# A two-model transformer stack on one core: part of its transposes done by VectorE's 32x32 transposes and DMA copies instead of by TensorE

## The reference, cut to what matters

```python
# first model, one layer
h = h + rmsnorm(mixed attention, convolution and pooling @ w_out)
m = rmsnorm(h, norm_mlp_pre[i])
m = jnp.square(jax.nn.relu(jnp.einsum('bsd,df->bsf', m, w_up[i])))     # 4096 wide
m = jnp.einsum('bsf,fd->bsd', m, w_down[i])
h = h + rmsnorm(m, norm_mlp_post[i])
h = h + sigmoid(h @ ple_gate[i]) * (p[i] @ ple_proj[i])

# second model, one layer
x = x + 0.5 * rmsnorm_2(swiglu(rmsnorm_2(x), ffn1_w_in, ffn1_w_out))   # 2816 wide
proj = u @ w_in                        # xa, ya, q, k, v, g, sb, sc, sh, gates
oa = (ha * jax.nn.gelu(ya)) @ w_lru_out
ret = retention(q, k, v, positions)    # 4 heads of 512 values, each normalised
ob = (jax.nn.silu(g) * ret) @ w_ret_out
oc = (sb * causal_depthwise_conv(sc * sh, sc_conv_w)) @ w_sc_out
mixture = (ga * oa + gb * ob + gc * oc) @ w_out
x = x + rmsnorm_2(mixture)
x = x + 0.5 * rmsnorm_2(swiglu(rmsnorm_2(x), ffn2_w_in, ffn2_w_out))
```

## Time and profile before

| | before |
|---|---|
| device time, median of 3 runs | 2320.12 us (2319.9 to 2321.6) |
| span of the profiled execution, first to last instruction | 2318.0 us |
| PE busy | 2296.8 us, 99% |
| weight loads (PEld) | 1959.9 us, 85% |
| VectorE busy | 1540.9 us, 66% |
| ScalarE busy | 1221.5 us, 53% |
| GpSimd busy | 79.1 us, 3% |
| DMA, share of 16 engines | 56.4% for the queue of SP's DMAs |
| mean granted TensorE clock | 0.999 |

### The profile page before, as it was taken

The page is one execution under the profiler, slowest core; times in us unless marked ns, Lnnn a source line. Parts: engine busy times, 40 slices in busy tenths (PEclk is TensorE's granted clock), DMA queues, the critical chain, the costliest instruction groups (busy, mean ns, idle before and its releaser), DMA issues.

```text
span 2318.0 us, 30390 instructions
## 1 busy us (share of the span) xinstructions
PE 2296.8 (99%) x12124; PEld 1959.9 (85%) x12124; DVE 1540.9 (66%) x2019; ACT 1221.5 (53%) x1788; POOL 79.1 (3%) x134
## 2 busy tenths in 40 slices
PE   8999999999999999999999999999999999999998
PEld 6888888888888888988888888888889888888887
DVE  6867657776566667876575665665678765756664
ACT  6645446464455556755444554554567553445553
POOL 0110000100000000000000000000000000000000
PEclk9999999999999999999999999999999999999999
DMA  8437655456656555645665465565556456554652
GB/s 334 146 119 238 198 171 209 146 170 203 211 163 217 189 172 163 206 162 183 218 199 191 157 217 192 179 221 190 173 164 214 153 183 221 195 193 164 199 193 89
DMA packets 119805, 434.91 MB, mean 188 GB/s; under 512 B 13553, under 2 KB 13809, under 8 KB 119665
## 3 DMA queue, kind: packets, MB, share of 16 engines
q1 hardware_dynamic: 119664, 432.96, 56.4%
HBM read 431.86 MB, written 1.05 MB: 187 GB/s over the span
## 4 chain that ended last, share of the span: by engine, by line
PE 95%; DVE 4%; ACT 1%; issue 0%; POOL 0%; DMA 0%; DVEq 0%; POOLq 0%; ACTq 0%
PE ub L1716 21%; PE ub L1713 11%; PE ub L1684 9%; PE ub L1686 9%; PE ub L1685 9%; PE acc L1684 8%; PE acc L1685 8%; PE acc L1686 8%; PE ub L1691 1%; PE ub L1692 1%; PE ub L1693 1%; PE acc L1747 1%; DVE wlo L1020 1%; DVE work L1208 1%; PE acc L2162 0%; DVE best L1205 0%
## 5 line engine op out<-in xcount | busy, mean ns | idle before, releaser
L1020 DVE TENSOR_TENSOR wlo<-raw,whi 128x1024 fp32r<-128x1024 f32 x776 | 913.1, 1220 | 215.2 <-ACT whi L534 213.4
L534 ACT ACTIVATE whi<-raw 128x1024 fp32r<-128x1024 f32 x776 | 777.3, 1052 | 200.9 <-PE ub L1686 140.5
L1716 PE MATMUL ub<-xhl,whi 128*128 128x512 f32 x2176 | 514.6, 390 | 0.0
L1716 PEld LDWEIGHTS ub<-xhl,whi 128*128 128x128 f32 x2176 | 404.2, 188 | 82.7 <-issue 1.3
L1684 PE MATMUL acc<-whi,bhl 128*128 128x512 f32 x736 | 288.2, 392 | 0.0
L1685 PE MATMUL acc<-wlo,bhl 128*128 128x512 f32 x736 | 286.6, 389 | 0.0
L1686 PE MATMUL acc<-whi,bhl 128*128 128x512 f32 x736 | 286.5, 389 | 0.0
L1684 PE MATMUL ub<-whi,xhl 128*128 128x512 f32 (+1 forms) x704 | 275.3, 391 | 3.0 <-DVE wlo L1020 1.5
L1713 PEld LDWEIGHTS ub<-xhl,wlo 128*128 128x128 f32 x2176 | 272.0, 191 | 6.2
L1713 PE MATMUL ub<-xhl,wlo 128*128 128x256 f32 x2176 | 275.4, 283 | 0.0
L1686 PE MATMUL ub<-whi,xhl 128*128 128x512 f32 (+1 forms) x704 | 272.5, 387 | 0.0
(11 more groups left out here) (305 smaller groups left out, 2471.7 us busy)
## 6 DMA issues: line engine op xcount, KB each, us to landing
raw<-in_w SPq DMA_DIRECT2D x776, 512.0 KB, 5.0
gain<-in_gains SPq DMA_DIRECT2D x20, 512.0 KB, 7.8
tapw<-in_taps SPq DMA_DIRECT2D x16, 512.0 KB, 4.3
DEC<-in_decay SPq DMA_DIRECT2D x2, 768.0 KB, 8.1
par<-in_par SPq DMA_DIRECT2D x2, 647.0 KB, 9.4
par<-in_par SPq DMA_DIRECT2D x2, 556.0 KB, 7.2
H<-in_x SPq DMA_DIRECT2D x2, 512.0 KB, 4.5
out_h<-H SPq DMA_DIRECT2D x4, 256.0 KB, 2.6
```

What stands on the lines that cost most here:

```text
L534: do(act.activation(whi[:, s % RING, c], raw[:, slot, c], ACT.Copy), counts["w_hi"])
L1020: do(dve.tensor_tensor(wlo[:, s % RING, c], raw[:, PLACES[s][0], c], whi[:, s % RING, c].bitcast(f32), ALU.subtract), counts["w_lo"])
L1716: last = pe.matmul(bank, whi[:, s % RING, n:n + P], xhl[:, kt, :, :].rearrange("p a n -> p (a n)"), start=first, stop=stop, skip_group_che ...
```

## The change

The three functions that had PE transpose a tile (`turn_first`, `turn_p`, and the call of `turn_m(0)`) are removed from PE's list. In their place:

- VectorE transposes the 32x32 blocks of each 128x512 tile (`to_blocks`), one instruction for a tile, from `FH` to `FB`, from `tX` to `PB`, or from `MIX` to `MB`, and counts a semaphore (`blocked` or `pb`).
- SP waits for that semaphore between two weight loads and issues 16 DMAs (`move`), one for each pair of 32-partition groups. Each moves 32 partitions by 128 columns (of one or of two tiles) from one partition group to another, so that the sixteen blocks of a 128x128 tile stand where a full transpose has them. They land in `FH`, `PD` or `MD`, and count 256 on `moved0` or `moved1`.
- ACT and VectorE split the result as before, but read it in SBUF, with the blocks in another order (`moved_blocks`, `by_blocks`).

The moves are: two in each of the six feed-forwards (t=0, t=1), four in each layer's retention, and one in each layer's mixture: 22 moves, 352 DMAs. VectorE has 36 new transposes. On ACT, `turned_p(hd)` stands one chunk later than before, behind the squares of the next head. `turn_m(1)` stays on PE. The diff, cut (the wait indices of the other calls and the same edits for the second feed-forwards are left out):

```diff
@@ -176,6 +176,7 @@
+        FB = sb("FB", 0, at=unit(56), shape=[P, 4, 512])
@@ -259,6 +260,10 @@
+        PB = sb("PB", 0, at=unit(48), shape=[P, 2, 2048])
+        PD = sb("PD", 0, at=unit(16), shape=[P, 2, 2048])
+        MB = sb("MB", 0, at=unit(56), shape=[P, 2, 512])
+        MD = sb("MD", 0, at=unit(60), shape=[P, 2, 512])
@@ -294,6 +299,17 @@
+        def in_blocks(t):
+            return t.rearrange("p (c q i) -> p q c i", c=4, i=32)
+        def moved_blocks(t):
+            return t.rearrange("p (a q i) -> p q a i", a=4, i=32)
+        def by_blocks(t):
+            return t.rearrange("p q (a i) -> p q a i", i=32)
@@ -332,6 +350,15 @@
+                def move(event, dst, src, landed):
+                    done[event] += 1
+                    sp.wait_ge(sem[event], done[event])
+                    for a_ in range(4):
+                        for c in range(4):
+                            sp.dma_start(dst[32 * c:32 * c + 32, :, cols(a_)],
+                                         src[32 * a_:32 * a_ + 32, :, cols(c)]).then_inc(sem[landed], 16)
@@ -386,6 +413,10 @@
                             load_taps(L, 2, PIECES)
+                        if s == s1(L, "ffn", 7):
+                            move("blocked", FH[:, 0:4:2, :], FB[:, 0:4:2, :], "moved0")
+                        if s == s1(L, "ffn", 9):
+                            move("blocked", FH[:, 1:4:2, :], FB[:, 1:4:2, :], "moved1")
                         if s == s1(L, "ffn", 10):
@@ -400,6 +431,17 @@
+                        for name in ("f1", "f2"):
+                            if s == s2(L, name + "first", 7):
+                                move("blocked", FH[:, 0:1, :], FB[:, 0:1, :], "moved0")
+                            if s == s2(L, name + "first", 9):
+                                move("blocked", FH[:, 1:2, :], FB[:, 1:2, :], "moved1")
+                        for hd in range(RET_HEADS):
+                            if s == s2(L, "g", 0) + 2 * hd + 6:
+                                vs = slice(hd * 512, (hd + 1) * 512)
+                                move("pb", PD[:, :, vs], PB[:, :, vs], "moved0")
+                        if s == s2(L, "sco", 1) + 7:
+                            move("blocked", MD[:, :, :], MB[:, :, :], "moved0")
@@ -575,12 +617,12 @@
-                def first_hi(pieces):
-                    for b, t in pieces:
-                        nxt("tr_done")
-                        do(act.activation(bhi[:, 4 * b:4 * b + 4, cols(t)], quad(acc[:, 2 * b + t, :]), ACT.Copy),
-                           counts["hh"])
+                def first_hi(t, blocks_):
+                    nxt(f"moved{t}", 256)
+                    for b in range(blocks_):
+                        do(act.activation(by_blocks(bhi[:, 4 * b:4 * b + 4, cols(t)]), moved_blocks(FH[:, 2 * b + t, :]),
+                                          ACT.Copy), counts["hh"])
@@ -896,12 +938,18 @@
+                        nxt("moved0", 256)
...
-                            nxt("tr_done")
-                            do(act.activation(bhi[:, 4 * hd:4 * hd + 4, cols(t)], quad(acc[:, 3 - t, :]), ACT.Copy),
-                               counts["rph"])
+                            do(act.activation(by_blocks(bhi[:, 4 * hd:4 * hd + 4, cols(t)]),
+                                              moved_blocks(PD[:, t, hd * 512:(hd + 1) * 512]), ACT.Copy), counts["rph"])
...
+                        if fb == 0:
+                            nxt("moved0", 256)
+                            for t in range(2):
+                                do(act.activation(by_blocks(bhi[:, 8:12, cols(t)]), moved_blocks(MD[:, t, :]), ACT.Copy),
+                                   counts["mh"])
+                            return
@@ -956,23 +1004,25 @@
                             hd = j // 2
-                            if j % 2 == 0:
-                                if hd:
-                                    turned_p(hd - 1)
-                            else:
+                            if j % 2:
                                 used(s)
+                                act.wait_ge(sem["pb"], RET_HEADS * L + hd)
                                 for t in range(2):
...
                                 squares_o(hd)
+                                if hd:
+                                    turned_p(hd - 1)
                         elif kind == "ya":
                             if j == 0:
-                                turned_p(RET_HEADS - 1)
+                                act.wait_ge(sem["pb"], RET_HEADS * (L + 1))
                             sums_out(j, s, j % 2)
...
                             do(act.activation(two(bhi, 16 + 2 * j), tX[:, j % 2, :], ACT.Copy), counts["hh"])
+                            if j == 1:
+                                turned_p(RET_HEADS - 1)
                         elif kind in ("gb", "ga", "gc") and j % 2:
@@ -1028,13 +1078,26 @@
-                def first_lo(pieces):
-                    for b, t in pieces:
+                def rest_of(t, u, source):
+                    return dve.tensor_tensor(by_blocks(blo[:, u:u + 4, cols(t)]), moved_blocks(source),
+                                             by_blocks(bhi[:, u:u + 4, cols(t)].bitcast(f32)), ALU.subtract)
+                def first_lo(t, blocks_):
+                    for b in range(blocks_):
...
-                        do(dve.tensor_tensor(blo[:, 4 * b:4 * b + 4, cols(t)], quad(acc[:, 2 * b + t, :]),
-                                             bhi[:, 4 * b:4 * b + 4, cols(t)].bitcast(f32), ALU.subtract),
-                           counts["hid"])
+                        do(rest_of(t, 4 * b, FH[:, 2 * b + t, :]), counts["hid"])
+                def to_blocks(dst, source, count=None):
+                    return do(dve.transpose(in_blocks(dst), source.rearrange("p (q c i) -> p q c i", c=4, i=32)), count)
+                def first_blocks(t, blocks_):
+                    settle()
+                    for b in range(blocks_):
+                        to_blocks(FB[:, 2 * b + t, :], FH[:, 2 * b + t, :], counts["blocked"] if b == blocks_ - 1 else None)
@@ -1311,13 +1374,15 @@
                                 first(1, 0)
+                                first_blocks(0, 2)
                                 lo(sf + 4)
...
                                 first(1, 1)
-                                first_lo(((0, 0), (1, 0)))
+                                first_blocks(1, 2)
+                                first_lo(0, 2)
                         elif kind == "up":
@@ -1492,17 +1559,21 @@
+                        settle()
+                        for t in range(2):
+                            to_blocks(PB[:, t, hd * 512:(hd + 1) * 512], tX[:, t, :], counts["pb"] if t else None)
...
-                            do(dve.tensor_tensor(blo[:, 4 * hd:4 * hd + 4, cols(t)], quad(acc[:, 3 - t, :]),
-                                                 bhi[:, 4 * hd:4 * hd + 4, cols(t)].bitcast(f32), ALU.subtract),
-                               counts["rx"])
+                            do(rest_of(t, 4 * hd, PD[:, t, hd * 512:(hd + 1) * 512]), counts["rx"])
...
+                            if fb == 0:
+                                do(rest_of(t, 8, MD[:, t, :]), counts["mx"])
+                                continue
@@ -1519,6 +1590,10 @@
                                    counts["mixed"] if final and t else None)
+                        if final and f == 0:
+                            settle()
+                            for t in range(2):
+                                to_blocks(MB[:, t, :], MIX[:, t, 0:512], counts["blocked"] if t else None)
@@ -1532,6 +1607,10 @@
                             continue
+                        if kind == "g" and j in (4, 6):
+                            turned_p(j // 2 - 2)
+                        elif (kind, j) in (("ya", 0), ("ya", 2)):
+                            turned_p(2 + j // 2)
                         if (kind == "g" and j in (2, 4, 6)) or (kind, j) == ("ya", 0):
@@ -1796,28 +1870,12 @@
-                    def turn_first(b, t):
-                        pe.wait_ge(sem["fp"], fp0 + (t if gated else 2 * t + b) + 1)
-                        A_[2 * b + t].take(pe, sem["hid"], hid0 + (2 * t + 1 if gated else 3 * t + b + 1))
-                        for q in range(4):
-                            last = pe.transpose(acc[:, 2 * b + t, q * P:(q + 1) * P],
-                                                FH[:, 2 * b + t, q * P:(q + 1) * P], ident)
-                        give(last, "tr_done")
...
-                        if kind == "first":
-                            if j == 3:
-                                for b in range(1 if gated else 2):
-                                    turn_first(b, 0)
-                        elif kind == "up":
+                        if kind == "up":
...
-                            if j == 4:
-                                for b in range(1 if gated else 2):
-                                    turn_first(b, 1)
```

(29 more changed lines are left out.)

19 lines of the change are left out of this document (8 added, 11 removed).

## The result

| | before | after |
|---|---|---|
| median | 2320.01 us (4 runs, 2319.45 to 2321.6) | 2344.93 us (4 runs, 2342.84 to 2350.94) |
| profiled execution | 2320.1 us | 2342.84 us |
| its span | 2318.0 us | 2341.1 us |

The ratio after to before is 1.0111, 95% interval [1.0096, 1.0125]. 2344.93 us lies outside the range of the prediction and on the other side of no change.

A forecast was written before the change was run, and what follows sets the result against it. PE's own list was taken as the bound (busy 2296.8 of 2318.0 us). The span less 15.9 us for removed transposes, nothing for contention or waits, gives 2302.1, plus 2.1 around it 2304.2 us; range 2300.7 to 2311.

The forecast's parts named there:

- What is removed: PE's list: 144 transposes go, in 14 groups of eight at 0.88 us and 8 of four at 0.45, 15.9 us.
- Transposes on VectorE: VectorE: 36 added transposes at 0.69 us each, 25 us beside 777 us of idle time.
- Contention: SBUF: copies running while PE reads it were put at nothing, upper end 3.6 us.
- The mixture: First half: weighing, transposes, move and split take 16.7 us of the 21.7 us that PE's four chunks last.
- A copy on SP: SP's queue: each copy costs 0.47 us to issue, from 0.43 to 0.99; sixteen hold SP 7.5 us.
- the text's own limit of 0.61: First model's down 0: the price per copy in us above which PE waits there.
- Landing: From a move's last issue until its data has landed: 2.6 us, upper end 5.0.
- Down 0: First model's feed-forward, t=1: VectorE's rests end at 178.4, PE arrives at 180.6; margin 2.2 us, so no wait.
- the text's formula: Both first-model feed-forwards together lose 32(p - 0.61) us at down 0, p being the price per copy.
- so the lateness does not add up: Retention: SP's 9.4 us of work for a head fits in the head's 14.4 us; PE sees no delay.
- SP becomes the bound: Rival, chance 0.09: copies cost SP 0.99 us each, feed-forwards lose 12.2 us and retention 12.4, giving 2328.8 us.
- The chance of 0.87 for faster: Whole kernel: 0.75 for the forecast case plus 0.12 for the gain partly given back.

The follow-up runs named there:

- one copy: The changed kernel with each move's sixteen copies made one DMA of the same bytes, without the exchange between partition groups: 2305.2 us, 0.9939.
- two queues: The changed kernel with eight of each move's sixteen copies issued from POOL, the others from SP: 2305.39 us, 0.9936.
- the feed-forwards alone: The changed kernel with only the six feed-forwards turned by VectorE and copies, retention and mixture by TensorE as before: 2328.43 us, 1.0034.
- the loop cut: The changed kernel with retention's rounding (ScalarE) and rests (VectorE) of a head put behind the next head's gated values and transposes: 2329.7 us, 1.0043.
- retention alone: The changed kernel with only retention's eight heads turned by VectorE and copies, feed-forwards and mixture by TensorE as before: 2340.33 us, 1.0089.

## Why the prediction was wrong, by its steps

- **What is removed** (15.9 us): right. 16.3 us by the ends of chunks, 14.9 net in the kernels without stalls (one copy, two queues).
- **Transposes on VectorE** (0.69 us): right, 0.69 to 0.70. **Contention** (nothing): right, as the one-copy and the two-queue kernel show. The mixture lost 1.2 us where the text had 5 us to spare.
- **A copy on SP** (0.47, upper end 0.99): measured 0.64, over the text's own limit of 0.61. It had been read from DMAs out of DRAM, which still cost 0.46; a copy from SBUF to SBUF costs more, and no row of before had one. **Landing** (2.6): 1.9, so this term was too dear.
- **Down 0, a margin of 2.2 us**: the failed step is "blocks are ready at 166.9, SP issues until 174.4". The blocks are ready at 166.6, but SP starts at 168.7 and issues until 179.2, since the first move and four loads stand ahead. The rests end at 182.5 instead of 178.4; 4.1 us late against 2.2 of margin is the wait of 2.0 us. By the text's formula 0.64 us a copy costs 32 x 0.03 = 1 us for both; it was 5.8 (3.80 and 1.98, the half clock behind the first included).
- **Retention**: the step that decided, "so the lateness does not add up". It compared SP's work for a head, 9.4 us, with the pace of 14.4. But SP does not start when it is free; it starts when VectorE has the next blocks, and VectorE stands behind the previous copies. The loop is 15p + landing + 4.86 us. At the text's own prices, 0.47 and 2.6, this is 14.5, already no less than the pace of 14.4, though 0.1 us a head alone would have cost little; at 0.64 and 1.9 it is 16.4, as measured, 2 us a head too long. It took both, the loop that was not seen and the price that was too low. All terms but the order of VectorE's list were in the text. The kernel with the order turned round loses 17 us less in retention, and the one with half the issues a queue keeps only 1.3 us of the 25.9.
- **The rival "SP becomes the bound"** (2328.8 us, chance 0.09) had the direction and the resource, with the wrong point: it decided from 0.94 us a copy on, by SP's own work. The 0.95 us for 64 KB that "DMA: Bandwidth & Descriptors" of the Trainium skill (section Bandwidth) measures is the transfer of a load from DRAM issued by GpSimd, not the price of an issue. Taken as a price per copy it gave 2322.1 us; the trace has 0.64 us an issue, and 512 KB cost SP about as much as 32 KB.
- **The clock**: in no term. A stall gave 2.9 us more in the sixteen matmuls behind ya 2 (6.74 against 3.81), and an estimated 1.7 us behind down 0 of the first layer (half of 3.4). Of the 39.6 us lost, PE's listed waits at the touched places (14.9 + 5.8 + 3.7 + 3.7, and 1.2 at the mixture) are 29.3; the rest, some 10 us, is the clock and refilling, a difference and not a measurement of its own.
- The chance of 0.87 for faster rested on one price with a margin of 2.2 us in a chain whose queue had not been followed.

## What to carry to other kernels

When work leaves the bounding engine for a round trip over queues, write the trip out as a loop: from one issue of it to the next, through every engine that keeps its order, and compare the sum with the pace, not each engine's load. A trip of many small DMAs is priced by its number, on the queue where it is issued, together with what stands ahead there; share it over two queues or make it fewer DMAs, and look at what the second queue's own engine has to do behind them. And put the wait for its return behind, not ahead of, the work that starts the next one.

## What the runs showed of the hardware

- SP issues a copy from SBUF to SBUF in 0.64 us (0.60 and a gap), of 16 or 32 KB alike; one of 512 KB is listed with 0.61 to 0.64. Eight reads of 64 KB from DRAM took it 0.46 each, four weight loads in a row behind a move 0.53 each.
- POOL issues the same copy in 0.54 us and in pieces of eight it lands after 1.8 us, but sixteen in a row hold a pause of up to 6.3 us (38.4 us over retention's eight moves, landing 2.7), eight at most one of 1.7 in the stretches read. The rule of the Trainium skill, "DMA: Bandwidth & Descriptors", section Issuing engine by pattern, that DMAs issued by Sync are generally faster than GpSimd's, holds here for sixteen (10.2 against 14.1 us), not for a single issue. What causes the pause was not tried.
- After stalls of PE of 1.9 to 2.7 us the granted clock sometimes fell for 3.4 us and sometimes not. At the same place, down 0 of the first layer, after 2.1 us in the kernel with the feed-forwards alone and after 2.2 us in the one with the loop cut, the window of 3 us reads 0.53 and 1.00 (column before the last two):

```profile
183.40:186.40 3.00, 3.00 (x10) 2.28 (x8) 2.97 (x5) 3.00 (x6) 0.00 (x0) 0.53 0.99 399
```

```profile
183.40:186.40 3.00, 3.00 (x13) 2.47 (x14) 2.97 (x4) 3.00 (x5) 0.00 (x0) 1.00 1.02 397
```

  With each of the stalls of 7 us read here it fell, for 6.8 us (retention alone) or 10.2 us (the changed kernel). In the changed kernel it fell with the 2.0 us at down 0 and stayed at 1.0 with the 2.2 us at gb 0 of the second layer and with all stalls of 1.9 us and less.
